# Weighted rows added up by the scatter, and half of the last expert matrix in rounded halves

## The reference

```python
def _moe_ffn(h, router_w, router_b, w1, w3, w2, sw1, sw3, sw2):
    scores = jax.nn.sigmoid((h @ router_w).astype(f32))
    ...
    _, idx = lax.top_k(sel, TOP_K)                      # 8 of 64 experts
    wts = jnp.take_along_axis(scores, idx, axis=1)
    wts = wts / jnp.sum(wts, -1, keepdims=True) * ROUTED_SCALE
    ...
    def body(acc, blk):
        tok, wt, e = blk                                # a block of 128 rows of one expert
        xb = h[tok]
        hid = jax.nn.silu(xb @ w1[e]) * (xb @ w3[e])
        return acc.at[tok].add(wt[:, None] * (hid @ w2[e]).astype(f32)), None
    ...
    shared = (jax.nn.silu(h @ sw1) * (h @ sw3)) @ sw2
    return routed.astype(h.dtype) + shared
```

## Time and profile before

| | us |
|---|---|
| median of 3 runs | 2884.3 |
| the three runs | 2882.22 to 2887.02 |
| the profiled execution | 2883.77 |
| its span (first to last instruction) | 2882.0 |
| TensorE busy in it | 2727.0 (95%) |
| VectorE busy | 1718.6 (60%) |
| ACT busy | 1161.9 (40%) |
| POOL busy | 215.3 (7%) |
| expert lists | about 742 to 786 |
| expert loop | about 783 to 1465 |
| combine | about 1465 to 1545 |
| attention starts in layer 1 and 2 | about 1711 and 2381 |

### The profile page before, as it was taken

The page is one execution under the profiler, slowest core; times in us unless marked ns, Lnnn a source line. Parts: engine busy times, 40 slices in busy tenths (PEclk is TensorE's granted clock), DMA queues, the critical chain, the costliest instruction groups (busy, mean ns, idle before and its releaser), DMA issues.

```text
span 2882.0 us, 42287 instructions
## 1 busy us (share of the span) xinstructions
PE 2727.0 (95%) x17110; PEld 2099.5 (73%) x17110; DVE 1718.6 (60%) x3109; ACT 1161.9 (40%) x2102; POOL 215.3 (7%) x212
## 2 busy tenths in 40 slices
PE   6998998889999999999988999999999998999998
PEld 6887767774766776666646766888888775788887
DVE  5256876666677777777646786432334688433333
ACT  3323553221365555565513338322223327432232
POOL 0000000000022122222200120000000030000000
PEclk9998998999999999999999989999999999999999
DMA  6210002424488989999975330324224240223321
GB/s 236 88 59 23 1 3 76 123 62 167 156 319 337 348 346 358 352 361 349 356 293 185 95 89 9 120 70 139 73 81 131 92 110 12 89 87 95 117 67 65
DMA packets 186543, 442.40 MB, mean 154 GB/s; under 512 B 21283, under 2 KB 110694, under 8 KB 167014
## 3 DMA queue, kind: packets, MB, share of 16 engines
q1 hardware_dynamic: 161862, 396.59, 38.3%
q0 software_dynamic: 24480, 43.04, 5.0%
HBM read 426.43 MB, written 38.29 MB: 161 GB/s over the span
## 4 chain that ended last, share of the span: by engine, by line
PE 80%; DVE 9%; DMA 5%; ACT 4%; issue 2%; SPq 0%; POOL 0%; ACTq 0%; DVEq 0%; POOLq 0%
PE ps L296 19%; PE ps L297 19%; PE ps L298 19%; PE ps L2522 6%; DMA ring<-in_ew 3%; PE ps L1519 2%; PE ps L2036 2%; PE ps L2548 2%; PE ps L2761 1%; PE ps L2240 1%; DVE Pb L3508 1%; DMA yr<-y_rows 1%; DVE spA L2458 1%; PE ps L3394 1%; PE ps L1854 1%
## 5 line engine op out<-in xcount | busy, mean ns | idle before, releaser
L2973 DVE TENSOR_TENSOR wf<-ring,wf 128x1024 fp32r<-128x1024 f32 (+1 forms) x152 | 181.6, 1196 | 312.0 <-ACT wf L2969 311.7
L2969 ACT ACTIVATE wf<-ring 128x1024 fp32r<-128x1024 f32 (+1 forms) x152 | 156.8, 1033 | 347.6 <-PE ps L298 347.6
L296 PE MATMUL ps<-hxh,wf 128*128 128x512 f32 (+1 forms) x736 | 279.9, 380 | 2.3 <-DVE hxl L3136 2.3
L297 PE MATMUL ps<-hxl,wf 128*128 128x512 f32 (+1 forms) x736 | 279.5, 380 | 0.0
L298 PE MATMUL ps<-hxh,wf 128*128 128x512 f32 (+1 forms) x736 | 279.5, 380 | 0.0
L2458 DVE TENSOR_TENSOR spA<-ring,spA 128x1024 fp32r<-128x1024 f32 x156 | 184.5, 1221 | 101.0 <-ACT spA L2453 100.8
L2522 PE MATMUL ps<-ring,hdT 128*128 128x512 f32 x520 | 234.8, 594 | 0.8 <-issue 0.8
L2453 ACT ACTIVATE spA<-ring 128x1024 fp32r<-128x1024 f32 x156 | 157.7, 1054 | 51.8 <-DMA ring<-in_ew 43.9
L2458 DVE TENSOR_TENSOR spB<-ring,spB 128x1024 fp32r<-128x1024 f32 x104 | 124.1, 1221 | 67.6 <-ACT spB L2453 64.9
L2522 PEld LDWEIGHTS ps<-ring,hdT 128*128 128x128 f32 x520 | 93.8, 190 | 94.3 <-issue 91.1
L296 PEld LDWEIGHTS ps<-hxh,wf 128*128 128x128 f32 x736 | 138.4, 188 | 28.9 <-DVE hxl L3136 2.8
(11 more groups left out here) (623 smaller groups left out, 6135.7 us busy)
## 6 DMA issues: line engine op xcount, KB each, us to landing
ring<-in_ew SPq DMA_DIRECT2D x65, 2048.0 KB, 12.1
ring<-in_ew SPq DMA_DIRECT2D x65, 1024.0 KB
ring<-in_w_in SPq DMA_DIRECT2D x17, 2048.0 KB, 8.0
ring<-in_w_gate SPq DMA_DIRECT2D x20, 1024.0 KB, 5.6
ring<-in_w_up SPq DMA_DIRECT2D x20, 1024.0 KB, 8.1
ring<-in_w_down SPq DMA_DIRECT2D x16, 1024.0 KB, 5.1
adaw<-in_ada_w SPq DMA_DIRECT2D x24, 512.0 KB, 6.5
ring<-in_w_out SPq DMA_DIRECT2D x6, 2048.0 KB, 8.2
```

The lines of the kernel that those rows point to most:

```text
L296: pe.matmul(o, lhs[0], rhs[0], start=start, stop=False)
L297: pe.matmul(o, lhs[0], rhs[1], start=False, stop=False)
L2969: act.activation(item_part(n)[0], item_raw(n), ACT.Copy).then_inc(*w_hi.inc(n))
L2973: v.tensor_tensor(item_part(n)[1], item_raw(n), f(item_part(n)[0]), ALU.subtract).then_inc(*w_lo.inc(n))
```

## The change

**Scatter that adds.** `y_rows` has 1024 rows instead of 4096: two arrays of 512 tokens, one for experts of even and one for experts of odd number, so that two neighbouring scatters never write one row. The scatter has `compute_op=ALU.add`. The arrays are cleared once by a POOL transfer of zeros from `hg`; the third gather and the first two scatters wait for it, and every later scatter waits until the one two before has landed. The routing weight is multiplied into the hidden tile: `val` carries it in three bf16 parts (`weight_parts`), `match_pe` delivers it for each slot (for the first group in 32 matmuls of their own, "Pw"), `slot_weights` adds the parts up to `wsl`, and L2592 becomes a `scalar_tensor_tensor` with it. `jr`, `j8`, `w8`, the diagonal matrices and the vector sums go; the combine loads 8 transfers of 512 KB, and TensorE adds with the identity: two matmuls for the shared expert's rows, four for the two arrays. SP's wait for the combine's loads ahead of the third load of `w_in` goes as well.

**Half of w2 in rounded halves.** The first 512 columns of w2 become a fifth piece (n, 4), split by ACT and VectorE like the others, and the hidden tile is split into `hdp`. Six `mm3` matmuls replace two full ones; the other 512 columns stay as they are, from `hdT`, now a single buffer. ACT alone evicts both banks (128x1024); VectorE's copy goes. Each piece has a fixed slot now, and its copy waits for the use of the same piece one expert before.

**Order of a step.** It is (4, 3, 1, 2, 0): the gathered rows are transposed ahead of the products. Piece 3 of the next expert is split behind the SiLU and the hidden tile. The list matmuls stand behind the products of every sixth step, and the list work of VectorE is spread over 60 steps.

**Attention.** Unit 0 no longer waits for `p_r`, the two banks' roles are swapped, and the rotation of blocks 17 and 18 is waited for at unit 16. The writing of the mask `zb` moves from the start of attention into the projection's last blocks.

```diff
-    yD = nc.dram_tensor("y_rows", (4096, D), F32, kind="Internal").ap()
+    yD = nc.dram_tensor("y_rows", (1024, D), F32, kind="Internal").ap()
...
+    def weight_parts(v, cols, w, left):
+        v.wait_ge(*V.val())
+        v.tensor_copy(val[:, :, cols, 3], w).then_inc(*V.inc())
+        v.wait_ge(*V.val())
+        v.tensor_tensor(left, w, val[:, :, cols, 3], ALU.subtract).then_inc(*V.inc())
+        v.wait_ge(*V.val())
+        v.tensor_copy(val[:, :, cols, 4], left).then_inc(*V.inc())
+        v.wait_ge(*V.val())
+        return v.tensor_tensor(val[:, :, cols, 5], left, val[:, :, cols, 4], ALU.subtract)
...
-        return [(k, s - k) for s in range(NX + 4) for k in (4, 3, 2, 1, 0) if k in parts and 0 <= s - k < NX]
+        return [(k, s - k) for s in range(NX + 4) for k in (4, 3, 1, 2, 0) if k in parts and 0 <= s - k < NX]
...
     def piece(e, j):
-        m = (4 * e + j) % 5
+        m = 2 if j == 4 else 4 if j == 2 and e else j
...
-                                    in_offset=None, bounds_check=4095, oob_is_err=False)
+                                    in_offset=None, bounds_check=1023, oob_is_err=False, compute_op=ALU.add)
...
+        g.dma_start(yD.rearrange("(a p) d -> p a d", p=128), bcm(hg[:, 2, :], 8)).then_inc(*d_zero.inc("in"))
...
+                if n == 2:
+                    g.wait_ge(*d_zero.val("in"))
                 gather(g, n, n % 3).then_inc(*d_gat.inc(n))
             else:
-                g.wait_ge(*k_dve.val(("y0", n)))
-                g.wait_ge(*k_act.val(("y1", n)))
+                g.wait_ge(*k_act.val(("y", n)))
+                g.wait_ge(*(d_sca.val(n - 2) if n >= 2 else d_zero.val("in")))
                 scatter(g, n, n % 3).then_inc(*d_sca.inc(n))
...
-                pe.wait_ge(*k_act.val(("hd", n)))
-                for q in range(2):
-                    if n:
-                        pe.wait_ge(*(k_act.val(("y1", n - 1)) if q else k_dve.val(("y0", n - 1))))
-                    for j in range(2):
-                        m = pe.matmul(ps[5 + q][:, :], hdT[:, n % 2, j, :], w2[:, j, q * 512:(q + 1) * 512], start=(j == 0), stop=(j == 1))
-                    m.then_inc(*k_pe.inc((f"y{q}", n)))
+                if n:
+                    pe.wait_ge(*k_act.val(("y", n - 1)))
+                pe.wait_ge(*k_dve.val(("hl", n)))
+                pe.wait_ge(*p_lo.val((n, 4)))
+                for j in range(2):
+                    m = mm3(pe, ps[5][:, :], [hdp[:, q, j, :] for q in range(2)], [w[:, j, :] for w in piece(n, 4)], start=(j == 0), stop=(j == 1))
+                m.then_inc(*p_use.inc((n, 4)))
+                pe.wait_ge(*k_act.val(("hf", n)))
+                for j in range(2):
+                    m = pe.matmul(ps[6][:, :], hdT[:, j, :], w2[:, j, 512:1024], start=(j == 0), stop=(j == 1))
+                m.then_inc(*k_pe.inc(("y1", n)))
...
-                v.tensor_tensor(hd2[:, n % 2, :], sl[:, n % 2, :], ps[2 + n % 2][:, 256:512], ALU.mult).then_inc(*k_dve.inc(("hd2", n)))
+                v.wait_ge(*l_dve.val(("ws", n // 8)))
+                v.scalar_tensor_tensor(out=hd2[:, n % 2, :], in0=sl[:, n % 2, :], scalar=wsl[:, n:n + 1], in1=ps[2 + n % 2][:, 256:512],
+                                       op0=ALU.mult, op1=ALU.mult).then_inc(*k_dve.inc(("hd2", n)))
...
-            else:
+            elif u == 1:
                 pe.wait_ge(*p_r.val((l, 18)))
-                if u:
-                    for c in (17, 18):
-                        pe.wait_ge(*rope_done(l, c))
+            if u == 16:
+                for c in (17, 18):
+                    pe.wait_ge(*rope_done(l, c))
```

More of the change, by code:

```diff
@@ L2139, in out_dve @@
             norm(2 * i + 1, h, x, g12[3][:, :], g12[2][:, :], e_xn.inc(i))
-        for i in range(4):
-            v.memset(val[:, i, :, 0], float(i)).then_inc(*V.inc())
-            v.tensor_scalar(val[:, i, :, 1], iota[:, 0:96], 0.0, C("ii"), ALU.mult, ALU.add).then_inc(*V.inc())
-        v.memset(val[:, :, :, 3], 1.0).then_inc(*V.inc())
         g8 = sel[:, :, :].rearrange("p i (g e) -> p (i g) e", g=8)
@@ L3859, in _ @@
         expert_dve(v)
-        diag_dve(v)
         over_dve(v)
```

259 lines of the change are left out of this document (125 added, 134 removed).

## The result

The changed kernel takes 2910.8 us (median of 4 runs, 2906.83 to 2918.17) against 2884.3 us before. The ratio is 1.0094, 95% interval 1.0072 to 1.0117: it is slower by 0.9%, where 0.8% faster was forecast, and it lies outside the range of 2836 to 2900. The profiled execution has a span of 2905.0 us.

A forecast was written before the change was run, and what follows sets the result against it. In the expert loop TensorE is full and the DMA engines nearly so; after the change DMA sets the step. Terms of -9 (loop), +2 (lists), +2 (loop end), -14.7 (combine), -4.2 (attention) make -24: 2860 us, range 2836 to 2900.

The forecast's parts named there:

- a share of 0.985: Expert loop: 10.10 us of DMA work divided by this share gives a step of 10.25 us, gain 9 us.
- Rival A: Expert loop: the added read costs no engine time, step 9.95 us, 2842 us in all; chance 0.17.
- Rival B: Scatter in each step: an added row costs more than twice a plain one, 2900 at two extra prices; chance 0.22.
- The deciding point: Expert loop: 15 us may be lost before the other gains are eaten; step 10.75 for level, extra of 1.15 us.
- Rival C: Expert loop: ACT and VectorE bind, 2872 us; weight buffers bind if loads land 2.5 us later; chance 0.13.
- the prediction's own sign: Expert loop: if steps are long while the DMA share is low, Rival C or Rival E holds.
- Rival D: Expert loop: bytes at 354 GB/s are the ceiling, step 11.1 us, 43 us lost, 2912; chance 0.04.
- Rival E: Expert loop: each scatter waits for the one two before; at 24 us the step is 12, about 2970; chance 0.04.
- The split of w2: Expert loop: TensorE saves 0.33 us a step, to 9.81, or 9.95 on average with the list steps.
- The lists: Expert lists: three-part rounding and 32 more list matmuls cost +2 us, bounds -1 and +6; the clearing costs nothing.
- The end of the loop and the combine: Last hidden tile costs +2 us; combine from last product takes 60 instead of 74.7 us, gain 14.7, bounds 9 and 20.
- Attention: Start of attention, both layers: the second unit's wait of 2.1 us goes, gain 4.2 us; moving the mask a little more.

The follow-up runs named there:

- e1: The changed kernel with a scatter that overwrites instead of adding, the sum over experts left out: 2846.2 us.
- e2: The kernel before with the split half of w2, the new step order and the attention edits; scatter, lists and combine as before: 2859.4 us.
- e10: The changed kernel, adding kept, loading only the first half of each w2, the other half stale: 2854.9 us.
- e7: The changed kernel adding only the first 512 of 1024 columns of each row, the experts' sum left out: 2839.7 us.
- e3: The kernel before with only an adding scatter into its 4096 rows, cleared first: step 11.11 us against 10.39.
- e6: The changed kernel with all of w2 as full matmuls again, adding kept: 2909.6 us.
- e12: e1 with one more plain transfer of 64 rows of 4 KB a step, issued by SP: 2931.4 us.
- e11: e2 with the step's old order, the gathered rows transposed behind the products again: 2920.8 us.
- e8: The kernel before with the attention edits alone: ratio 0.9967 (0.9955 to 0.9978).

## Why the prediction was wrong

**The step that failed** is in the expert loop: "so I allow a share of 0.985". The work that the share was to divide was nearly right: forecast 10.10 us a step. Measured in the changed kernel it is (75.2% + 17.7%) x 11.01 = 10.23. Of that the adding has 0.63, where 0.65 was forecast, and queue 0 took 1.95 us a step (17.7% of 11.01), as much as the 19% of 10.25 that was to show the forecast right. The Trainium skill (Collectives: The Full Stack, "Why ReduceScatter is half of AllGather") has 32 against 62 GB/s for a transfer that reads two sources; the doubled row of e1 against the changed kernel agrees with it. But the share was 0.93, and 10.23 / 0.93 = 11.0. The 0.985 was my choice, from the combine's 1.01 at 418 GB/s, a stretch of plain loads with no gathers or scatters beside them. The loop's own rows had 0.91 and 0.92, with ACT already waiting for weights; no row showed this mix of transfers at more.

The kernels lay this out, share times step being the work:

| kernel | step, us | DMA share | work a step, us | who sets the step |
|---|---|---|---|---|
| e2, split, no adding | 10.01 | 0.91 | 9.1 | TensorE |
| e10, adding, light load | 10.16 | 0.90 | 9.1 | TensorE |
| e7, half rows added | 9.98 | 0.93 | 9.3 | TensorE |
| e1, changed, no adding | 10.05 | 0.93 | 9.3 | TensorE |
| before | 10.39 | 0.91 | 9.5 | TensorE |
| e3, before, adding | 11.11 | 0.89 | 9.9 | loads and TensorE in turn |
| e6, adding, w2 not split | 11.08 | 0.92 | 10.2 | loads |
| after | 11.01 | 0.93 | 10.2 | loads |
| e12, plain extra rows | 11.35 | 0.94 | 10.7 | loads |

No kernel of the loop went over 0.94, whoever set the step. At 0.93 a step of 10.05 has room for 9.35 us of work, and e1 uses 9.3: the split had taken the last room, and adding came on top.

This does not make 0.93 a ceiling of the engines. The packets in the trace show what the missing 0.07 is. In the changed kernel all sixteen engines are at work for 70% of 820 to 1440, and nine tenths of their idle time lie in stretches, 14% of the time in all, in which 9 work on average. These stretches lie around SP's issue of w2: in the microsecond behind it 9.5 engines are busy in the mean, two microseconds later all sixteen. Before the change it is the same (16% of the time; 8.7 engines). What SP waits for, changed kernel, 820 to 1440:

```profile
SPq L2504 <- PE ps L2546: 428.5, 49, 9.6
SPq L2497 <- DVE spB L2475: 86.4, 53, 2.7
```

So the queues run dry while SP waits for TensorE's last matrix before it issues w2, and the share of 0.93 is at least in part made by the order of SP's list and the two buffers. It is the factor that was wrong, and the table shows it for this list; a kernel with w2's load elsewhere, or a third buffer, is the rival that no run tests. The mean share also hides that a scatter's rows are not on all engines: the last one's 44 rows took 3.3 us at 328 ns each, mostly three at a time. And for 23% of 820 to 1440 (before the change 7%) one to four packets of a 2 MB load are still under way while eight or more of the next 1 MB load are. So a few engines run late, which may be what makes loads land late; the trace does not name the engines, and this stays open too.

**Rival A** (the read costs no engine time): it costs 0.63 us a step. **Rival B** named the right place and mechanism (loads behind the scatter land late, ACT's splits wait, TensorE stands), and the result looks like it. But its condition, an extra price over 1.15 us, was not met: 0.63 was enough. The deciding point was worked out with the same 0.985, and with a slip: 15 us over 61 steps are 0.25, so a step of 10.65 for the level and not 10.75. With 0.93 it would have been where work passes 0.93 x 10.65 = 9.9, an extra of 0.45 over 9.45, and the forecast's own 0.65 lies above that. What it held against B, 4 KB rows at 418 GB/s, was misread: nine tenths of the bytes in that stretch are packets of 8 KB.

**Rival C** (ACT and VectorE): e6 shows nothing of it, and e2 holds 10.01 with both of them as full. Its second half, the buffer loop, is what the chain now shows: loads land 3.9 us later, and 2.5 was its condition. But it is a symptom, since e1 has the same loop without the loss. By the prediction's own sign (long steps while the share is low) C or E should hold; what held of it is only this.

**Rival D** (bytes are the ceiling, 354 GB/s) gave 2912, the closest number of all, for a chance of 0.04. It is not shown. With the read of an add counted (0.26 MB a step, 24 GB/s), the changed kernel moves 356 GB/s and e3 346; but e12, as late, moves 343 in all, and e1 moves 361 without being late. The Trainium skill's about 358 GB/s of HBM for a core (DMA: Bandwidth & Descriptors, "Specifications", half of a stack's 716) is passed by e1 by a little and by the combine before by far (418). Share and bytes go together in most of these kernels, so the table can't tell them apart; that the idle time sits around one issue in each step speaks against a ceiling in bytes, but does not exclude one.

**Rival E**: a scatter lands after 16.5 us, still under two steps (22.0); its wait was free (between 820 and 1440 POOL waits for no landing).

**The split of w2**: forecast 9.81 and 9.95 with list steps, measured 10.01 and 10.05, full TensorE. Right, and so was the reading that the order of the step buys it; e11 puts a number to that, 0.91 us a step, where I had counted a spare of 0.3.

**The lists**: forecast +2 with bounds to +6, measured +5.4 to the indices. The first product starts 6.4 us later against the mask (790.4 and 746.6 for 786.1 and 748.7), and the 24 of the first expert end 4.9 later, so part is given back, as was said. VectorE, changed kernel, timeline:

```profile
779.16 0.29 DVE L2363 TENSOR_SCALAR rk<-ps 128x128 f32<-128x128 f32 x1 [8.49 <-PE ps L2284]
779.48 0.58 DVE L2372 CAST val<-ps 128x128 bf16<-128x128 f32 x1
780.10 0.32 DVE L2374 TENSOR_TENSOR wov<-ps,val 128x128 f32<-128x128 f32 x1
780.46 0.38 DVE L2376 CAST val<-wov 128x128 bf16<-128x128 f32 x1
780.87 0.59 DVE L2378 TENSOR_TENSOR val<-wov,val 128x128 bf16<-128x128 f32 x1
```

The three-part rounding takes 2.0 us here where one copy of 0.4 stood, and the other 4 us had come before 779.16 (32.6 us behind the mask, 28.6 before): hardly any of it was hidden behind the shared expert. The clearing cost nothing, as said: its 4 MB are through before the third gather is due.

**The end of the loop and the combine.** From the last hidden tile's transposes to the last product's end it is 8.7 us for 4.7 before: +4 where +2 was forecast, among others because the last `mm3` products take 0.43 us each instead of 0.23 (the granted clock is 0.80 from 1507 to 1512, behind TensorE's wait for the split). Chain of the changed kernel, and the last tile's L3126 in VectorE's timeline, against the earlier trace rows:

```profile
1510.79 1.03 ACT yb L2584
...
1512.58 8.27 DMA y_rows<-yb,idx
1520.93 4.07 DMA yr<-y_rows
1525.04 5.88 PE ps L2784 x8
```
```profile
1570.91 1.28 DVE L3126 SCALAR_TENSOR_TENSOR xn<-xt,rmv,grow 128x1024 f32<-128x1024 f32 x1
```

60.1 us from 1510.79, where 60 was forecast. That it is so near is luck, since three terms are off and cancel: the adding scatter takes 8.3 instead of 5.0 us, the first loads 4.1 instead of 6.8, and the first passes 5.9 instead of 6.75. The mechanism, VectorE as the chain behind the first tile, is as described: a tile takes 9.8 to 10.8 us.

**Attention**: right in kind and mis-sized, 8.6 to 9.5 for 4.2. Second unit, both layers, changed kernel, and the second layer's row of before:

```profile
1739.56 0.28 DVE L3507 CUSTOM_DVE_ANT_0 Pb<-ps,zb 128x128 f32<-128x128 f32 x1
...
2405.30 0.28 DVE L3507 CUSTOM_DVE_ANT_0 Pb<-ps,zb 128x128 f32<-128x128 f32 x1
```
```profile
2382.29 0.29 DVE L3508 CUSTOM_DVE_ANT_0 Pb<-ps,zb 128x128 f32<-128x128 f32 x1 [2.10 <-PE ps L3384]
```

The wait of 2.10 us is gone in both. From the combine's last L3129 or L3126 to that unit it is 168.7 us for 172.6, and from layer to layer 665.7 for 670.3; behind it nothing changes (499.7 both). So each layer gains 4.0 to 4.6: 2.1 for the wait, and as much again ahead of the first unit, where the mask's two writes (0.6 us) stood on VectorE's path and the first unit waited for block 18; no run takes these two apart. That part was priced at "a little".

Put together from single runs of each part: -9.5 (e8), -14.6 (combine), +5.4 (lists), -22 (loop without adding, 64 x (10.05 - 10.39)), +64.5 (adding, all stages) is +24, against +26.5 by the medians; the price of adding holds the last scatter's, which the combine's term holds too.

The best version that came out of it is e2, 2859.4 us, 0.9% faster than before: it takes the split half of w2 and the attention edits and leaves the scatter as it was.

## What to carry to other kernels

Two resources near full must be read together: if TensorE is at 99% and the DMA engines at 0.92 beside it, the room of the second is what the first may be sped up by, and nothing else may be put on it. Plan with the share that this very mix of transfers shows, not with one from another stage, and before calling it a limit look where in a step the engines are idle and which wait in the issuing engine's list stands there. Work that saves bytes at the end (here 12 MB of reads in the combine, 14.6 us) is dear if it is paid in every step of a loop that is full (0.6 us of engine time in each of 65 steps came to 64 us).

## What was not expected of the hardware

- An added row costs its DMA engine twice a plain one, by the byte: 330 ns for 4 KB where a plain one takes 159 (changed kernel and e1), and 180 ns for 2 KB (e7).
- The loss is larger than the engine time that causes it. 0.63 us of adding gave 0.96 us a step (11.01 against 10.05), and 0.64 us of plain rows (e12) gave 1.30. The load packets themselves took longer: 8.28 us a step against 8.04 with the same bytes in the first case, 82.1% of 11.35 = 9.32 less the 0.64 of the rows, 8.7, in the second. Why they do is not shown.
- The adding scatter of the last block, beside a load of 512 KB and nothing else, landed after 8.27 us where a plain one took 3.73 before the change and 4.30 in e1.
